# Strassen's seven products in the second matmul of an MLP too, in a two-layer diffusion step

## The chip, the cores and the metric

The kernel runs on one core of a Trainium2 chip. The metric is the device time of one execution in microseconds (us); lower is better. All inputs lie in HBM, all outputs end there.

## What is computed

Two trunk layers over 640 tokens (512 latent, 128 context) of width 1024. Layer 0 mixes by a convolution module and a bidirectional retention, layer 1 by grouped-query attention. Behind each mixer stands the part that the change touches:

```python
h = rmsnorm(x, norm_g[layer, 1]) * (1 + sc2) + sh2
x = x + g2 * (jnp.square(jax.nn.relu(h @ mlp_w1[layer])) @ mlp_w2[layer])
```

`mlp_w1` is 1024 x 4096 and `mlp_w2` 4096 x 1024, all in fp32. `sh2`, `sc2` and `g2` come from `silu(c) @ ada_w[layer]` and differ between latent and context tokens.

## The kernel before

Everything is held transposed: features on the 128 partitions, tokens along the free dimension, in two halves of 320 (`HALF`). An fp32 matmul is made of three in the reduced format `fp32r`: each operand is split into a high part (a rounding copy, by ScalarE) and a low part (value minus high part, by VectorE or GpSimd), and TensorE adds high x high, high x low and low x high in PSUM.

**Groups.** `mlp` works through the 4096 hidden features in 8 groups of 512 (`CYCLES`). A group's first matmul makes 512 hidden features from `h`, then ReLU and square, and its second matmul adds their product with 512 rows of `mlp_w2` to `x`. Groups 1 and 2 (`PLAIN`) do both in the ordinary way. In groups 3 to 8 the first matmul is a Strassen-like scheme (Winograd's form) of seven products of half-size blocks (`winograd`, line 1092 its matmul): the weights split in four blocks B11 to B22, the tokens in two halves, the 1024 input features in two. Three of its weight operands are blocks, four are sums of blocks (T1 to T4), made by VectorE in `t_sums` (line 2354) from the four loaded blocks; their high parts come from `split_product` (ScalarE, L1351) and their low parts from `t_lo` (VectorE, L2360). Each product is two output tiles of 128 x 320 with 4 chunks of 128 and 3 matmuls, 12 matmuls a tile. Products are combined in `combine` and `result` (VectorE, L2366); `product_1` (ScalarE, L1637) copies the first out of PSUM. `hidden_pair` (ScalarE, L1643 to L1651) does ReLU, square and high part per tile, `hidden_lo` (VectorE, L2298) the low part.

The second matmul of every group is plain: 16 output tiles x 4 chunks x 3 = 192 matmuls of 320 columns (`product`, line 665), each tile added to `xT` with the gate by `residual` (VectorE, L1876).

**Weights.** Raw weights come in blocks of 128 x 1024 fp32 (512 KB) by loads that SyncE issues (`load_mlp`, `load_tile`), into two pairs of buffers, `raw` and `raw_high`. `wH` and `wL` are rings of four blocks: the high part of a block may be written once TensorE is done with the block four before it. The order of `BLOCKS` is the order of use. Low parts of blocks that are not sums are made by GpSimd (`lo`, L1840), two instructions of 512 columns each.

**Order.** Each engine runs its own queue in written order and waits for semaphores: `acc_full` counts finished output tiles, `dve_free` tiles that VectorE has read, `wh_done`, `wl_done` and `t_low` weight parts. An instruction that waits holds up all behind it on its engine. In layer 0 TensorE also runs three strips of 32 small matmuls per group (`strips`, L784) for the modulation of later stages; each needs a load of 1 MB (`load_ada`), and VectorE's `modulation` finishes every second one.

The loop that sets the order of the second matmul:

```python
for q in range(4):
    w = weights((t + 2 + q // 2, q % 2), 256)
    for j in range(4):
        half, m = j // 2, j % 2
        free(4 * q + j)
```

Of the kernel before, what the change touches and what calls it, by code (L numbers as in the profile page):

```python
# [82 lines left out]
RAW_HIGH = [t for t in range(N_TILES) if t % 2 and t in TWO_RAW]  # L83
RAW_LOW = [t for t in range(N_TILES) if t not in RAW_HIGH]
RAW_AT = {t: (tiles, n) for tiles in (RAW_LOW, RAW_HIGH) for n, t in enumerate(tiles)}


def WINO_OF(t):

    for layer, t0 in enumerate((T_MLP0, T_MLP1)):  # L90
        c, b = divmod(t - t0, 4)
        if PLAIN <= c < CYCLES and b < 2:
            return WINO * layer + c - PLAIN, b
    return None


B11, T2, B21, T3, T1, T4, B22 = range(7)
T_ORDER, SUM_ORDER = (T2, T3, T1, T4), (T3, T1, T2, T4)
BLOCKS = []
for t_ in range(N_TILES):  # L100
    if WINO_OF(t_) is None:
        BLOCKS += [(t_, 0), (t_, 1)]
    elif WINO_OF(t_)[1] == 0:
        BLOCKS += [("p", WINO_OF(t_)[0], i_) for i_ in range(7)]
BLOCK_AT = {key: n for n, key in enumerate(BLOCKS)}
POOL_LO = [key for key in BLOCKS if (key[2] not in T_ORDER if key[0] == "p" else key[0] not in DVE_LO)]
# [11 lines left out]
G_CYCLE = [24 * c + 6 * max(c - PLAIN, 0) for c in range(CYCLES + 1)]  # L118
# [6 lines left out]
A_MLP1 = A_QKV + 30  # L125
def F_AT(c, half, k):

    if c == 0:
        return 4 * half + k
    if c < PLAIN:  # L130
        return 4 * (k // 2) + 2 * half + k % 2
    return k + (4 if (half == 0) == (k < 2) else 0)


F_GROUP = [{F_AT(c, half, k): (k, half) for half in range(2) for k in range(4)} for c in range(CYCLES)]

# [8 lines left out]
V_WO = V_MLP0 + 16 * CYCLES  # L145
# [79 lines left out]
def hybrid_step(nc, x_prompt, x_sample, state_ret, cache_k, cache_v, ada_w, even_w_in, even_w_out, final_g,  # L225
# [3 lines left out]
    with ctx:  # L229
# [3 lines left out]
        def place(name, shape, dt=F32):  # L233
# [70 lines left out]
        here[0] = arena  # L304
        fH = place("fH", [P, 4, T], F32R)
        fL = place("fL", [P, 4, T], F32R)
        fr = place("fr", [P, 4, HALF])
        fs = place("fs", [P, 2, HALF])
# [3 lines left out]
        p1 = place("p1", [P, 2, HALF])  # L312
        u2 = place("u2", [P, 2, HALF])
        u3 = place("u3", [P, 2, HALF])
        s1_raw = nc.alloc_sbuf_tensor_at("s1_raw", [P, 4, HALF], F32, offset=mlp_end)
        s23 = place("s23", [P, 2, 2, 4, HALF], F32R)
        s4_raw = place("s4_raw", [P, 4, HALF])
        s4 = place("s4", [P, 2, 4, HALF], F32R)
        t1_raw = nc.alloc_sbuf_tensor_at("t1_raw", [P, 1024], F32, offset=here[0] - 4 * 3840)
# [3 lines left out]
        t3_raw, t2_raw, t4_raw = (nc.alloc_sbuf_tensor_at(f"t{n}_raw", [P, 1024], F32, offset=norm_buffers + 4096 * j)  # L323
                                  for j, n in enumerate((3, 2, 4)))
# [44 lines left out]
        t_raw = {T1: t1_raw, T2: t2_raw, T3: t3_raw, T4: t4_raw}  # L369
        s_hi = {1: hH[:, 0:4, 0:HALF], 2: s23[:, 0, 0], 3: s23[:, 1, 0], 4: s4[:, 0]}  # L370
        s_lo = {1: hL[:, 0:4, 0:HALF], 2: s23[:, 0, 1], 3: s23[:, 1, 1], 4: s4[:, 1]}
# [10 lines left out]
        def raw(t):  # L382

            return raw_high if t % 2 and t in TWO_RAW else raw_low
# [11 lines left out]
        def sem(name):  # L396
# [7 lines left out]
        raw_in = [sem("raw_in0"), sem("raw_in1")]  # L404
        raw_high_in = [sem("raw_high_in0"), sem("raw_high_in1")]
# [33 lines left out]
        t_sum, t_low = sem("t_sum"), sem("t_low")  # L439
        p1_done, u2_done, u3_done, w5_done, c_done = (sem("p1_done"), sem("u2_done"), sem("u3_done"), sem("w5_done"),  # L440
                                                     sem("c_done"))
# [14 lines left out]
        def raw_landed(t, j):  # L456

            return (raw_high_in if RAW_AT[t][0] is RAW_HIGH else raw_in)[j]

        def wait_raw(engine, t, j):  # L460

            engine.wait_ge(raw_landed(t, j), 16 * (RAW_AT[t][1] + 1))

        def wait_low(engine, *key):

            if key[0] == "p" and key[2] in T_ORDER:
                engine.wait_ge(t_low, 4 * key[1] + T_ORDER.index(key[2]) + 1)
# [7 lines left out]
        def wait_raw_free(engine, t, j):  # L475

            if WINO_OF(t) is None:
                wait_low(engine, t, j)
            else:
                s, odd = WINO_OF(t)  # L480
                engine.wait_ge(t_sum, 4 * s + 4)
                if (odd, j) != (1, 0):
                    wait_low(engine, "p", s, (B11, B21, None, B22)[2 * odd + j])
# [5 lines left out]
        def _(sp):  # L489
# [3 lines left out]

            def load_tile(t, halves, js=(0, 1)):

                for j, src in enumerate(halves):
                    tiles, at = RAW_AT[t]
                    if j in js:
                        if at:
                            wait_raw_free(sp, tiles[at - 1], j)  # L500
                    else:
                        continue
                    n = src.shape[2]
                    sp.dma_start(raw(t)[:, j, :].rearrange("p (k n) -> p k n", n=n), src).then_inc(raw_landed(t, j), 16)
# [69 lines left out]
            def load_mlp(layer, first_tile):  # L574
# [15 lines left out]

                w1(0)
# [2062 lines left out]
```

## Time and profile before

| | |
|---|---|
| median of 3 runs | 1569.06 us (1567.79 to 1569.22) |
| profiled execution: its time and span | 1567.7 us |
| mean granted TensorE clock | 0.997 of full speed |
| TensorE, VectorE, ScalarE, GpSimd busy | 1546.4, 989.9, 625.7, 487.8 us |
| HBM traffic | 162.23 MB, 103 GB/s in the mean |

The span runs from the first to the last instruction of one profiled execution; the profiled execution's own time is this span, 1567.7 us, 1.4 below the median of the runs. Matmuls overlap: a single one shows as 309 ns while the next starts 147 ns after it, so the cost of a stage is read from its length, not from the sum of its instructions. Likewise a VectorE or ScalarE instruction may start somewhat before its predecessor's shown end.

### The profile page before, as it was taken

The numbers are of one execution on the slowest core, as the hardware profiler recorded it, in microseconds if no ns is written. First come the engines' busy times: TensorE is split into PE (matmuls) and PEld (weight loads), VectorE is DVE, ScalarE is ACT, GpSimd is POOL, SyncE is SP. The second block draws the span as 40 slices with busy tenths as digits, with TensorE's granted clock in tenths as the row PEclk, the third lists the DMA queues.
The fourth block names the chain that finished last, engine by engine and source line by source line (L and its number), as shares of the span: only waits on it lengthen the run. The fifth ranks groups of instructions, "written<-read, shape, count | busy, mean of one in ns | idle before, by whom it ended". The sixth has DMA issues, their size and how long they took to land.

```text
span 1567.7 us, 28794 instructions
## 1 busy us (share of the span) xinstructions
PE 1546.4 (99%) x11994; PEld 1513.1 (97%) x11994; DVE 989.9 (63%) x1831; ACT 625.7 (40%) x1152; POOL 487.8 (31%) x350
## 2 busy tenths in 40 slices
PE   8999999999999999999999999999999999999998
PEld 7999999999999999999999999999999999999998
DVE  5348678675774755565555888773675755556555
ACT  5323333344432344234235534652443334523443
POOL 0233313314222343143235253101333344324431
PEclk9999999999999999999999999999999999999999
DMA  9454333313243334344253121001221232223212
GB/s 330 154 180 151 116 114 123 101 55 108 81 151 116 124 124 139 116 135 149 95 161 134 35 81 61 28 2 54 81 81 55 67 108 68 82 68 102 74 54 82
DMA packets 133410, 162.23 MB, mean 103 GB/s; under 512 B 4640, under 2 KB 108064, under 8 KB 133280
## 3 DMA queue, kind: packets, MB, share of 16 engines
q1 hardware_dynamic: 132048, 159.34, 31.5%
q8 instruction: 95, 1.56, 0.4%
q10 hardware_dynamic: 1232, 1.05, 0.2%
q14 instruction: 35, 0.29, 0.1%
HBM read 156.44 MB, written 3.93 MB: 102 GB/s over the span
## 4 chain that ended last, share of the span: by engine, by line
PE 90%; DVE 6%; ACT 2%; issue 1%; DMA 0%; POOL 0%; DVEq 0%; ACTq 0%
PE ps L665 59%; PE ps L1092 19%; PE ps L784 3%; PE ps L1284 2%; PE ps L1232 1%; DVE ps L1915 1%; PE ps L921 1%; PE ps L954 1%; DVE hL L1926 1%; PE ps L870 1%; DVE ps L1905 1%; PE ps L950 1%; DVE amx L2512 1%; ACT wH L1328 1%; PE ps L1259 1%
## 5 line engine op out<-in xcount | busy, mean ns | idle before, releaser
L1840 POOL TENSOR_TENSOR wL<-raw,wH 128x512 fp32r<-128x512 f32 x212 | 314.6, 1509 | 709.5 <-ACT wH L1328 514.7
L665 PE MATMUL ps<-fH,wH 128*128 128x320 f32 x1024 | 318.5, 311 | 0.2 <-DVE fL L2298 0.2
L665 PE MATMUL ps<-fL,wH 128*128 128x320 f32 x1024 | 316.3, 309 | 0.0
L665 PE MATMUL ps<-fH,wL 128*128 128x320 f32 x1024 | 316.3, 309 | 0.0
L1876 DVE SCALAR_TENSOR_TENSOR xT<-ps,modT,xT 128x192 f32<-128x192 f32 (+1 forms) x456 | 183.3, 434 | 192.0 <-PE ps L665 190.1
L1840 POOL TENSOR_TENSOR wL<-raw_high,wH 128x512 fp32r<-128x512 f32 x124 | 164.2, 1349 | 338.5 <-ACT wH L1351 209.6
L665 PE MATMUL ps<-hH,wH 128*128 128x320 f32 x704 | 221.1, 314 | 1.9 <-DVE hL L1926 1.3
L665 PE MATMUL ps<-hH,wL 128*128 128x320 f32 x704 | 217.5, 309 | 0.0
L665 PE MATMUL ps<-hL,wH 128*128 128x320 f32 x704 | 217.5, 309 | 0.0
L665 PEld LDWEIGHTS ps<-fH,wH 128*128 128x128 f32 x1024 | 192.3, 188 | 3.4 <-DVE xT L1876 1.2
L665 PEld LDWEIGHTS ps<-fL,wH 128*128 128x128 f32 x1024 | 192.3, 188 | 0.1
L665 PEld LDWEIGHTS ps<-fH,wL 128*128 128x128 f32 x1024 | 192.3, 188 | 0.0
L665 PE MATMUL ps<-wH,hH 128*128 128x256 f32 x560 | 162.1, 289 | 2.4 <-DVE hL L1926 2.1
L665 PE MATMUL ps<-wL,hH 128*128 128x256 f32 x560 | 158.3, 283 | 0.0
L665 PE MATMUL ps<-wH,hL 128*128 128x256 f32 x560 | 158.3, 283 | 0.0
L1351 ACT ACTIVATE wH<-t_raw 128x1024 fp32r<-128x1024 f32 x48 | 50.8, 1059 | 226.6 <-PE ps L665 172.9
L665 PEld LDWEIGHTS ps<-hH,wH 128*128 128x128 f32 x704 | 132.2, 188 | 6.4 <-DVE hL L1926 2.8
L665 PEld LDWEIGHTS ps<-hL,wH 128*128 128x128 f32 x704 | 132.2, 188 | 0.2
L665 PEld LDWEIGHTS ps<-hH,wL 128*128 128x128 f32 x704 | 132.1, 188 | 0.0
L2298 DVE TENSOR_TENSOR fL<-fs,fH 128x320 fp32r<-128x320 f32 x128 | 92.0, 749 | 58.8 <-ACT fH L1651 52.3
L1092 PE MATMUL ps<-s,wH 128*128 128x320 f32 x576 | 127.9, 310 | 0.0
L1092 PE MATMUL ps<-hH,wH 128*128 128x320 f32 x384 | 119.3, 311 | 0.0
(271 smaller groups left out, 3095.4 us busy)
## 6 DMA issues: line engine op xcount, KB each, us to landing
ada<-in_ada_w SPq DMA_DIRECT2D x40, 1024.0 KB, 5.3
raw<-in_mlp_w SPq DMA_DIRECT2D x64, 512.0 KB, 3.7
raw_high<-in_mlp_w SPq DMA_DIRECT2D x64, 512.0 KB, 3.8
raw<-in_even_w_in SPq DMA_DIRECT2D x28, 512.0 KB, 5.9
pre_w<-in_ada_w SPq DMA_DIRECT2D x16, 512.0 KB, 8.9
raw<-in_odd_w_qkv SPq DMA_DIRECT2D x10, 512.0 KB, 3.5
raw<-in_even_w_out SPq DMA_DIRECT2D x8, 512.0 KB, 3.5
raw<-in_odd_w_o SPq DMA_DIRECT2D x6, 512.0 KB, 3.4
```

Source lines behind the costliest of these rows:

```text
L665: last = nc.tensor.matmul(ps[:, bank, 0:width], a_, b_, start=(k == 0 and p_ == 0), stop=(k == nk - 1 and p_ == 2))
L784: last = nc.tensor.matmul(ps[32 * j:32 * j + 32, B_ADA, 0:P], siluc[:, 4 * part + k, :], by_lane[:, j], start=(part == 0 and k == 0), stop ...
L870: last = nc.tensor.matmul(ps[:, GATE_BANKS[n], 0:HALF], a_, b_, start=(k == 0 and p_ == 0), stop=(k == KC - 1 and p_ == 2))
L921: return nc.tensor.matmul(ps[:, bank, at:at + RV], kd_nat[:, r, tile, :], v_nat[:, tile, :], start=True, stop=True)
L950: last = nc.tensor.matmul(out, prob[:, cs], v_nat[:, tile, :], start=True, stop=ctx_)
L954: last = nc.tensor.matmul(out, qdec[:, r, cs], S[:, r, n, :], start=False, stop=(r == 1))
L1092: last = nc.tensor.matmul(ps[:, bank + m, 0:HALF], a_, b_, start=(k == 0 and p_ == 0), stop=(k == 3 and p_ == 2))
L1284: last = nc.tensor.matmul(ps[:, 6, cs], va[:, vt, kv * P:(kv + 1) * P], pT[:, h % 2, n, cs], start=(n == 0), stop=(n == 4))
L1351: nc.scalar.activation(wH[:, BLOCK_AT["p", s, i] % 4, :], src, ACT.Copy).then_inc(wh_done, 1)
L1840: last = nc.gpsimd.tensor_tensor(wL[:, at % 4, cs], raw(t)[:, j, cs], wH[:, at % 4, cs].bitcast(F32), ALU.subtract)
L1876: last = nc.vector.scalar_tensor_tensor(out=x, in0=ps[:, n % 4, c0 - half * HALF:c0 - half * HALF + w_], scalar=modT[:, gate_at + k, which ...
L2298: nc.vector.tensor_tensor(fL[:, k, halfcols(half)], fs[:, n % 2, :], fH[:, k, halfcols(half)].bitcast(F32), ALU.subtract).then_inc(f_ready, 1)
```

## The change

In groups 3 to 7 of both layers (`W2`) the second matmul becomes seven products too (`second_strassen`). The group's 512 hidden features and the 1024 outputs are halved, and so are the tokens. Four weight sums T1 to T4 of `mlp_w2` blocks are made by VectorE (`q_add`), four sums of hidden blocks S1 to S4 likewise (`operand_sum`), and each of the seven hidden operands gets a high part (`operand_hi`, ScalarE) and a low part (`operand_lo`, VectorE) in a ring `fx` of three. All instructions on hidden blocks now work on 640 columns at once. Products are accumulated on each other in the same PSUM bank: TensorE adds products one to four in banks 0 to 3, and VectorE reads each bank in between (`product_out`), before the next product is added to it. For one token half the reading goes straight to `xT`, for the other into a buffer `held` over all five groups, which group 8 adds to `xT` (`held_out`).

The first matmul of groups 3 to 8 (`first_strassen`) accumulates its products likewise. Its weight sums are no longer made by VectorE: GpSimd issues loads that add to what lies in the buffer (`accum_op`), five per group, T2 and T4 in a buffer of their own, T1 and T3 in raw buffers. All low parts of second-matmul blocks, and those of B11, T2 and T3 of the first, are GpSimd's; T1, B22, B21 and T4 are VectorE's. The raw buffers become one ring of four within the MLPs. `operand_hi` of the fourth to seventh operand waits until TensorE is done with the operand three before.

```diff
-B11, T2, B21, T3, T1, T4, B22 = range(7)
+W2 = range(PLAIN, CYCLES - 1)
+B11, T2, T3, T1, B22, B21, T4 = range(7)
+Q_ORDER = (B11, T2, T3, T4, T1, B22, B21)
+P_DVE = (T1, B22, B21, T4)
...
+            def block_product(key, width, nk, bank, m, operand, opens):
+                w = weights(key, width)
+                for k in range(nk):
+                    (aH, aL), (bH, bL) = [x[:, k, m * P:(m + 1) * P] for x in w], operand(k)
+                    for p_, (a_, b_) in enumerate(((aH, bH), (aH, bL), (aL, bH))):
+                        last = nc.tensor.matmul(ps[:, bank, 0:HALF], a_, b_, start=(opens and k == 0 and p_ == 0),
+                                                stop=(k == nk - 1 and p_ == 2), skip_group_check=not opens)
+                last.then_inc(acc_full, 1)
...
+            def second_strassen(layer, c, v, part):
...
+                def begin(i, name):
+                    wait_low(pe, "q", s, i)
+                    pe.wait_ge(x_low, 7 * s + name + 1)
+                begin(B11, A11_)
+                for m in range(4):
+                    if m < 3:
+                        pe.wait_ge(c_done, 6 * s1 + 3 + m)
+                    one(B11, A11_, m, m)
+                begin(T2, S2_)
+                for m in range(4):
+                    pe.wait_ge(dve_free, v + m + 1)
+                    one(T2, S2_, m, m, False)
...
+            # ScalarE, a group with both matmuls by seven products
+                        partials(c, p1, 1, p1_done)
+                        split_product("p", s, B22, g + 2)
+                        partials(c, u2, 3, u2_done)
+                        split_product("p", s, B21, g + 4)
+                        partials(c, u3, 5, u3_done)
+                        split_product("p", s, T4, g + 6)
+                        split_product("q", s2, B11, g + 8)
+                        hidden_block(c, F11)
+                        operand_hi(c, A11_)
+                        split_product("q", s2, T2, g + 10)
+                        hidden_block(c, F21)
+                        operand_hi(c, S3_)
+                        hidden_block(c, F22)
+                        split_product("q", s2, T3, g + 12)
+                        operand_hi(c, S2_)
+                        hidden_block(c, F12)
+                        split_product("q", s2, T4, g + 14)
+                        operand_hi(c, A22_)
...
+                        for n, i in enumerate((B11, T2, T3, T1)):
+                            split_product("p", s + 1, i, g + 30 + 4 * n)
...
+            # GpSimd
+            def add_block(s, out, row, col, done):
+                layer, c = s // WINO, PLAIN + s % WINO
+                src = mlp_w1[layer, 512 * row:512 * (row + 1), 512 * c + 256 * col:512 * c + 256 * (col + 1)]
+                nc.gpsimd.dma_start(out.rearrange("p (k n) -> p k n", n=256), src.rearrange("(k p) n -> p k n", p=P),
+                                    accum_op=ALU.add).then_inc(done, 16)
+            def t1_ends(s):
+                wait_raw(pool, "p", s, T1)
+                add_block(s, raw(("p", s, T1)), 0, 0, t1_added)
...
+                    after[before[0]] = lambda s=s: t2_begins(s)
+                    after[before[1]] = lambda s=s: t2_ends(s)
+                    after[before[2]] = lambda s=s: t3_ends(s)
+                    after["p", s, B11] = lambda s=s: t1_ends(s)
+                    after["p", s, T2] = lambda s=s: t4_ends(s)
...
+            # VectorE
+                def strassen_cycle(c):
+                    t_lo(s, T1)
+                    t_lo(s, B22)
                     modulate(c, 0)
+                    t_lo(s, B21)
+                    q_add(s2, T1)
                     t_lo(s, T4)
+                    combine(c, F11, 0)
+                    combine(c, F11, 1)
+                    modulate(c, 1)
+                    q_add(s2, T2)
+                    combine(c, F21, 0)
+                    operand_lo(c, A11_)
+                    combine(c, F21, 1)
+                    q_add(s2, T3)
+                    combine(c, F22, 0)
+                    operand_sum(c, S3_)
+                    combine(c, F22, 1)
+                    q_add(s2, T4)
+                    operand_lo(c, S3_)
+                    operand_sum(c, S2_)
+                    operand_sum(c, S1_)
+                    operand_lo(c, S2_)
+                    for m in range(4):
+                        product_out(c, 0, m)
+                    product_out(c, 1, 0)
+                    operand_lo(c, A22_)
...
```

Here `q_add` of T4 waits for `wait_raw` of B21 and for GpSimd's low part of T2 (`wait_low(dve, "q", s2, T2)`), since it overwrites the buffer of T2. `F11`, `F21`, `F22`, `F12` are the four blocks of hidden features by token half.

## Rows read from the trace of the kernel before

**Rows 1.** The page: busy time, share of the span and instructions; granted clock by slices.
```profile
PE 1546.4 (99%) x11994; PEld 1513.1 (97%) x11994; DVE 989.9 (63%) x1831; ACT 625.7 (40%) x1152; POOL 487.8 (31%) x350
...
PEclk9999999999999999999999999999999999999999
```

**Rows 2.** The page: chain that ended last, shares by line.
```profile
PE ps L665 59%; PE ps L1092 19%; PE ps L784 3%; PE ps L1284 2%; PE ps L1232 1%; DVE ps L1915 1%; PE ps L921 1%; PE ps L954 1%; DVE hL L1926 1%; PE ps L870 1%; DVE ps L1905 1%; PE ps L950 1%; DVE amx L2512 1%; ACT wH L1328 1%; PE ps L1259 1%
```

**Rows 3.** Chain in order of time, one group of layer 0: start, us, what.
```profile
678.54 14.07 PE ps L665 x96
692.62 1.01 PE ps L784 x32
693.63 14.28 PE ps L665 x96
```

**Rows 4.** The same, one group of layer 1.
```profile
1237.52 24.64 PE ps L1092 x168
1262.15 28.28 PE ps L665 x192
```

**Rows 5.** Busy time by stage; columns: stretch, length, engines, clock, DMA share, GB/s.
```profile
651.50:678.54 27.04, 27.04 (x234) 26.26 (x234) 14.87 (x26) 15.01 (x27) 8.12 (x6) 1.00 0.41 141
622.13:651.50 29.37, 29.37 (x226) 28.98 (x226) 16.64 (x33) 6.45 (x10) 10.70 (x8) 1.00 0.41 123
...
1262.15:1290.43 28.28, 28.28 (x195) 28.28 (x195) 16.31 (x32) 6.51 (x11) 10.72 (x8) 1.00 0.30 93
1237.52:1262.15 24.63, 24.63 (x169) 24.53 (x169) 14.23 (x23) 14.87 (x27) 8.13 (x6) 1.00 0.23 76
```

**Rows 6.** VectorE in order of time: start, us, instruction; 1024, 1280, 320 columns.
```profile
602.08 1.22 DVE L2360 TENSOR_TENSOR wL<-t_raw,wH 128x1024 fp32r<-128x1024 f32 x1
603.43 0.49 DVE L2366 TENSOR_TENSOR u<-ps,p 128x320 f32<-128x320 f32 x1
...
630.97 0.55 DVE L1876 SCALAR_TENSOR_TENSOR xT<-ps,modT,xT 128x320 f32<-128x320 f32 x1 [1.08 <-PE ps L665]
...
1205.35 1.48 DVE L2318 TENSOR_TENSOR s_raw<-hH,hL 128x1280 f32<-128x1280 f32 x1
```

**Rows 7.** ScalarE: a high part of a block, and two copies of 320 columns.
```profile
617.57 1.05 ACT L1328 ACTIVATE wH<-raw 128x1024 fp32r<-128x1024 f32 x1
...
623.20 0.81 ACT L1647 ACTIVATE fs<-fr 128x320 f32<-128x320 f32 x2
```

**Rows 8.** GpSimd in order of time: pairs of halves, alone and beside VectorE.
```profile
1182.14 2.56 POOL L1840 TENSOR_TENSOR wL<-raw_high,wH 128x512 fp32r<-128x512 f32 x2 [4.50 <-ACT wH L1328]
...
645.64 3.07 POOL L1840 TENSOR_TENSOR wL<-raw,wH 128x512 fp32r<-128x512 f32 x2 [12.76 <-ACT wH L1351]
```

**Rows 9.** GpSimd and VectorE in the same stretch, subtractions with both inputs in SBUF.
```profile
1196.90 6.37 POOL L1840 TENSOR_TENSOR wL<-raw,wH 128x512 fp32r<-128x512 f32 x4 [12.21 <-ACT wH L1328]
...
1199.07 1.54 DVE L2307 TENSOR_TENSOR fs<-fr 128x320 f32<-128x320 f32 x1 [1.23 <-ACT fr L1628]
...
1202.04 2.58 DVE L2318 TENSOR_TENSOR s_raw<-s_raw 128x1280 f32<-128x1280 f32 x1
1204.54 0.48 DVE L2307 TENSOR_TENSOR fs<-fr 128x320 f32<-128x320 f32 x1
```

**Rows 10.** TensorE's next tile starts, and VectorE reads the tile before.
```profile
606.68 0.46 PE L1092 MATMUL ps<-s,wH 128*128 128x320 f32 x2
...
606.95 0.49 DVE L2366 TENSOR_TENSOR fr<-ps,p 128x320 f32<-128x320 f32 x1 [0.87 <-PE ps L1092]
```

**Rows 11.** Loads: count, KB each, median us to landing; and SyncE's issue.
```profile
ada<-in_ada_w SPq DMA_DIRECT2D x40, 1024.0 KB, 5.3
raw<-in_mlp_w SPq DMA_DIRECT2D x64, 512.0 KB, 3.7
...
raw_high<-in_even_w_in SPq DMA_DIRECT2D x4, 512.0 KB, 9.0
...
613.28 0.37 SPq L504 DMA_DIRECT2D raw_high<-in_mlp_w  x1
```

More of the change, by code:

```diff
@@ L82 @@
 TWO_RAW = {T_GATE + 1, T_VAL + 1, *range(T_WC - 2, T_QKV + 2), *range(T_WO + 2, N_TILES)}
[L83 to L94, printed above, removed]
@@ new lines @@
+for t_ in range(N_TILES):
+    layer_ = 0 if T_MLP0 <= t_ < T_QKV else 1
+    c_, b_ = divmod(t_ - (T_MLP0, T_MLP1)[layer_], 4)
+    if not (T_MLP0 <= t_ < T_QKV or T_MLP1 <= t_) or b_ < 2 and c_ < PLAIN or b_ > 1 and c_ not in W2:
+        BLOCKS += both(t_)
+        RAW_SEQ += both(t_)
+    elif b_ == 0:
+        BLOCKS += [("p", WINO * layer_ + c_ - PLAIN, i_) for i_ in range(7)]
+        RAW_SEQ += [("p", WINO * layer_ + c_ - PLAIN, i_) for i_ in (B11, T3, T1, B22, B21)]
+    elif b_ == 2:
+        BLOCKS += [("q", len(W2) * layer_ + c_ - PLAIN, i_) for i_ in Q_ORDER]
+        RAW_SEQ += [("q", len(W2) * layer_ + c_ - PLAIN, i_) for i_ in (B11, T1, B22, B21)]
@@ L125 @@
 A_MLP1 = A_QKV + 30
+F_CYCLE = {0: 0, 1: 8, CYCLES - 1: 16}
+F_LAYER = 24
 def F_AT(c, half, k):
@@ L492, in cols, with load_raw @@
                 return w[k0 * P:(k0 + nk) * P, bass.ds(c0, n)].rearrange("(k p) n -> p k n", p=P)
+            def load_raw(key, src):
+                if RAW_PREV[key]:
+                    wait_raw_free(sp, RAW_PREV[key])
+                sp.dma_start(raw(key).rearrange("p (k n) -> p k n", n=src.shape[2]), src).then_inc(raw_landed(key)[0], 16)
             def load_tile(t, halves, js=(0, 1)):
[L496 to L504, printed above, removed]
+                for j in js:
+                    load_raw((t, j), halves[j])
             def k8(w, c0, row0=0):
@@ new lines, in partial, with partials @@
+                def partial(c, m, out, groups, done):
+                    act.wait_ge(acc_full, g0 + G_CYCLE[c] + groups + m)
+                    nc.scalar.activation(out[:, m, :], ps[:, 6 + m, 0:HALF], ACT.Copy).then_inc(done, 1)
+                def partials(c, out, groups, done):
+                    s, s2 = WINO * layer + c - PLAIN, len(W2) * layer + c - PLAIN
+                    if out is p1 and c == PLAIN:
+                        act.wait_ge(s_ready, 4 * layer + 4)
+                    elif out is p1:
+                        act.wait_ge(c_done, 6 * s)
+                    elif out is u3 and c - 1 in W2:
+                        act.wait_ge(x_low, 7 * (s2 - 1) + S4_ + 1)
+                    for m in range(2):
+                        partial(c, m, out, groups, done)
@@ new lines, in combine @@
+                def combine(c, b, m):
+                    s = WINO * layer + c - PLAIN
+                    bank, add, done, op = ((m, u3, u3_done, ALU.subtract), (m, u2, u2_done, ALU.subtract),
+                                           ((2, 5)[m], p1, p1_done, ALU.add))[b]
+                    dve.wait_ge(acc_full, g0 + G_CYCLE[c] + 7 + 2 * b + m)
+                    dve.wait_ge(done, 2 * s + 1 + m)
+                    nc.vector.tensor_tensor(fq[:, b, m, :], ps[:, bank, 0:HALF], add[:, m, :], op).then_inc(c_done, 1)
@@ new lines, in held_out @@
+                def held_out(k):
+                    for c0, w_, which in SEGS[1]:
+                        x = xT[:, k, c0:c0 + w_]
+                        nc.vector.scalar_tensor_tensor(out=x, in0=held[:, k, c0 - HALF:c0 - HALF + w_],
+                                                       scalar=modT[:, gate_at + k, which:which + 1], in1=x,
+                                                       op0=ALU.mult, op1=ALU.add)
+                def strassen_cycle(c):
+                    s, s2 = WINO * layer + c - PLAIN, len(W2) * layer + c - PLAIN
+                    t_lo(s, T1)
+                    t_lo(s, B22)
```

607 lines of the change are left out of this document (388 added, 219 removed).

## The prediction

> **What bounds the kernel now.** I read the busy shares and the clock first, then the chain that ended last, then that chain group by group, then the tables by stage, and only then single queues. TensorE is busy for 99% of the span at the full granted clock, 2.4 GHz [rows 1], and 78% of the chain are matmuls of the two product helpers [rows 2]. An MLP group of layer 0 is TensorE from end to end: 27.04 us for the first matmul (168 matmuls and two 1.01 us strips), 29.37 for the second (192 and one strip), 56.4 in all [rows 3, 5]; in layer 1 it is 24.63 + 28.28 = 52.9 [rows 4]. In both TensorE is busy for the whole length [rows 5]: it waits for nothing. VectorE is busy 14.9 to 16.6 us per half group, ScalarE 15.0 and 6.5, GpSimd 8.1 and 10.7, the DMA engines 0.41 in layer 0 and 0.23 to 0.30 in layer 1 [rows 5]. So TensorE work taken out is time, as far as the others keep up; the prediction is about them. The profiled span, 1567.7, lies 1.4 us below the median of the runs, 1569.06; I subtract from the median.
>
> **What is removed on TensorE.** A matmul of 320 columns costs 24.63 / 168 = 0.147 us [rows 4]. A second matmul by seven products is 7 x 4 output tiles x 2 chunks x 3 = 168 matmuls, not 192: 24 fewer, 3.52 us, in ten groups: 35.2 us. The 0.1 to 0.2 us by which 192 matmuls exceed 192 x 0.147 (14.28 against 14.08 for 96 [rows 3]) I let go too: 1.6 in all. The first matmul keeps 14 groups of 12 matmuls (1.76 us each); the second gets 28 of 6 (0.88 each, 3.52 per product). Floor with all else hidden: 1569.1 - 36.8 = 1532.3, some 24.64 + 24.64 = 49.3 us per group in layer 1 and 52.3 in layer 0.
>
> **What the other engines get.** Prices: VectorE 1.22 us for 1024 columns and 1.48 for 1280, both inputs in SBUF, so 0.82 for 640; 0.49 for 320 out of PSUM; 0.55 for a residual update; each starts about 0.07 before its predecessor's end [rows 6]. ScalarE 1.05 for 1024, 0.455 for 320, so 0.72 for 640 [rows 7]. GpSimd 1.27 for half a weight block [rows 8].
> - VectorE per group: four low parts and four sums of second weights (8 x 1.15), four operand sums and seven operand low parts (11 x 0.75), six combinations and 28 products out (34 x 0.44): 32.4 us plus 0.5 of modulation, of 49.3. The sums T1 to T4 of the first matmul (4 x 1.15) go. It fits as a sum.
> - ScalarE: 14 x 0.96 + 6 x 0.37 + 15 x 0.64 = 25.3 us. It fits.
> - GpSimd: ten blocks, not seven: 25.4 us, plus five issues of adding loads. The first to last of these ten have about 12 block times of 3.52 us = 42.
> - A bank is read while three other banks are written (2.64 us); a read takes 0.5, so accumulating on the read bank costs nothing while VectorE is not over 2 us late.
> - In the last group the held half goes out as 16 small updates, some 5.5 us of VectorE beside a first matmul in which it has over 9 us free: nothing. The swapped halves of the S operands, the ring of raw buffers, the rope loads' earlier release and the other banks have the same cover; I cost them at nothing, and at up to 1 us in all if not.
>
> **The wait that I expect.** VectorE's 320-column subtraction takes 0.48 us, but 1.54 beside GpSimd's, and the 1280-column one 2.58, not 1.48; GpSimd's four halves then take 6.37, not 5.1 [rows 9]. They take turns: one half block of GpSimd (1.1 us of waiting) between any two such VectorE instructions. Instructions that read PSUM and one SBUF operand don't wait. Until now the two hardly meet; the changed group has 19 such VectorE instructions against 20 halves, and seven of the nineteen stand in one chain. I walked the queues in their written order with these prices, 0.27 us from a group's end to its reader [rows 10], 1.3 us per issue on GpSimd. Time from the start of a layer 1 group: the second phase starts at 24.6, product two (T2 with S2) is due at 28.2. The F22 tiles end at 21.1, but VectorE is late by then: the low part of A11 waited for a half block (18.2 to 19.0), T3's sum ends at 20.6, S3's sum waits for a half and runs 21.6 to 22.4, so F22 is combined at 22.9. Relu and square: 24.6. T4's sum needs GpSimd's low part of T2 (23.6): to 24.9. Low part of S3: 25.6. Sum S2: 26.4. GpSimd's half; sum S1, queued ahead: 27.4 to 28.2. GpSimd's half; low part of S2: 30.0. Product one's first bank is read behind it, until 30.4, and the second product must wait for that too: 30.4 against 28.2 is 2.3 us (unrounded). The same walk without turns has S2 ready at 26.5, 1.6 us early, and stalls nowhere. In layer 0, with VectorE's modulation (0.5) in the same queue every other group, it gives 2.3 to 2.6. Ten groups: 5 x 2.3 + 5 x 2.45 = 23.8.
>
> On this the Trainium skill has a rule (SBUF - State Buffer, "Who interferes with whom"): a VectorE instruction with two SBUF inputs contends with a GpSimd instruction that reads SBUF, and who holds the port blocks the other. It speaks against this change, and the rows agree: 0.48 against 1.54. Without the rule the time would be the floor.
>
> **The adding loads.** No row has a load issued by GpSimd or one that adds; the bounds are rows of others. *Issue*: from below SyncE's 0.37 us [rows 11]; from above a slowed pair of halves, 3.07 [rows 8]; I take 1.3, the nearest, one GpSimd instruction. *Landing from the start of the issue*: plain 512 KB take 3.7, or 9.0 in the crowded head stage, a 1 MB load 5.3 [rows 11]. An adding load handles its bytes twice, so 1.3 + 5.3 = 6.6, between 3.7 and 1.3 + 9.0 = 10.3. What waits: ScalarE's high part of T1 (first matmul) stands ahead of its copies of product one, and those free the bank for TensorE's third tile. T1's add is issued when the low part of B11 is done, some 4 to 6 us before the new group; it may land up to 2 us into it. Landing at 6.6 costs nothing in the walk, 8 costs 0.9 per layer 1 group, 10 costs 2.9 (layer 0 1.2, its strip being cover). GpSimd's queue waits too, before three of the five adds: for the plain load under T3 and under T1, which SyncE may issue only when the low part of the block that held the buffer is done, and for the first add under T2. In the walk these have landed 0.5 to 3 us before GpSimd comes to them. SyncE passes two MB loads of the modulation in layer 0 between them; each waits for a strip that TensorE has run by then, and none of its waits is longer than one block time. All this leans on GpSimd being on time: a late block delays the next raw load, and that the add. Traffic: a group loads 15 half megabytes, not 8; layer 0's 7.3 MB at share 0.41 become 11, share 0.62, and 0.8 if added bytes count twice. That is below one but stretches landings.
>
> The Trainium skill says that a DMA's add needs two source reads, which halves the rate (Collectives: The Full Stack, "The bandwidth ceiling"), and gives about 1 us to the first byte for loads issued by GpSimd (DMA: Bandwidth & Descriptors, "Specifications"). No row here shows either; they would leave my landing, and lower the issue to about 1.0.
>
> By issue (and landing) the stalls per group in layer 1 and 0 come to: 0.4 (3.7): 1.2 and 1.9; 1.3 (6.6): 2.3 and 2.45; 2.0 (6.6): 2.9 and 3.8; 2.5 (8): 5.6 and 5.1; 3.0 (9): 10.2 and 8.6.
>
> **The sum.** 1569.1 - 36.8 + 23.8 = 1556.1. I say 1556.
>
> **Rivals.**
> 1. *Forecast*: turns at the port, late S2, 1.5 to 3 us in each of ten groups: 1547 to 1563. Chance 0.40.
> 2. *All hidden*: the turns are shorter than in rows 9 or fall elsewhere; the walk without them has 1.6 us to spare. For it: TensorE has no waits now. Against: rows 9. 1532 to 1547, centre 1534. Chance 0.27.
> 3. *GpSimd becomes the bound* (slower). Five issues and ten blocks in one queue; from its T4 block (free to start 3.2 us into the second phase) to the low part of T3 it has 28.5 us for seven blocks and four issues: 7 x 2.6 + VectorE's turns of 4 + 4 issues. It decides from an issue of 2.1 us or a landing over 9: then T1 lands late, ScalarE stands, and TensorE waits in every group. At 2.5 and 8: 1569.1 - 36.8 + 53.5 = 1586; at 3.0 and 9: 1626. For it: 3.07 us is a price that pairs of halves reach. Against: issues elsewhere cost 0.37. Chance 0.26, and 0.07 more for cases between, 1563 to 1572.
>
> **Numbers.** A measurement of this kernel tells about 0.2%, 3 us, from no change. Faster by more (under 1566): 0.40 + 0.27 + 0.02 = 0.69; within: 0.06; slower: 0.25. For 8 in 10 the range takes in all of the first two and the slow case up to an issue of 2.4: 1533 to 1582; the forecast's own is 1547 to 1563.
>
> **What would show it.** Second matmul, layer 1: 168 matmuls and one gap of 2 to 2.5 us ahead of product two's first tile, released by VectorE's reading of product one (line of the product read); its low part of S2 ends 5 us after the phase starts. VectorE's 640-column subtractions spread from 0.82 to 1.9 us. GpSimd busy over 25 us per group, each issue near 1.3. If the gap is not there, the turns were mispriced; if a gap stands ahead of the third tile of a group, released by ScalarE's copy, it is rival 3. A TensorE wait on weights in most groups, or on a read in the later products, would make the working wrong.

## The result

Before: 1569.1 us. After: 1624.6 us median (1609.1 to 1635.8), ratio 1.033 [1.029, 1.036]: slower by 3.3%, outside the predicted range (1533 to 1582), 69 us above the forecast of 1556. Here and below the medians are of all runs and the ratios of the fast ones alone; without the slow run of 1635.8 us the median after is 1620.0. The profiled execution took 1620.0 us, of which its span, the stretch from the first to the last instruction, is 1617.8. (In its later executions the kernel before takes 1.8 us more than its span as well, so the 1567.7 us of its profile are a span and not also a time; the prediction subtracts from the median, and nothing in it changes.)

The page of the kernel after: busy time, the queue of the loads that GpSimd issues (packets, MB, share), the chain by engine, and two rows of issues (KB each, median us to landing).
```profile
PE 1540.4 (95%) x11754; PEld 1498.7 (93%) x11754; DVE 1128.9 (70%) x1829; ACT 683.0 (42%) x1140; POOL 648.8 (40%) x470
...
q0 software_dynamic: 31680, 31.46, 13.1%
...
PE 68%; DVE 15%; ACT 6%; POOL 4%; DMA 4%; issue 3%; DVEq 0%; SPq 0%; ACTq 0%
...
t_first<-in_mlp_w POOLq DMA_DIRECT2D x36, 512.0 KB, 6.2
raw_high<-in_mlp_w POOLq DMA_DIRECT2D x14, 512.0 KB, 7.7
```
Against [rows 1, 2]: 240 matmuls are gone, as said, but TensorE's busy time fell by 6.0 us only, not by 35, and its share from 99 to 95%. The span less TensorE's busy time, 21.3 us before (1567.7 - 1546.4), is now 77.4. VectorE has 15% of the chain.

Layer 1, kernel after; columns as in [rows 5]: a whole group, then the first matmul of the next one, and the stretch of its second in which a long stall lies.
```profile
1325.20:1380.60 55.40, 52.05 (x340) 51.14 (x339) 42.54 (x54) 26.91 (x35) 34.49 (x26) 0.97 0.64 143
1380.60:1405.20 24.60, 24.21 (x165) 23.98 (x164) 15.78 (x16) 12.39 (x18) 8.23 (x7) 1.00 0.64 153
1405.20:1435.70 30.50, 22.91 (x137) 22.42 (x136) 27.22 (x32) 13.34 (x17) 20.83 (x16) 0.89 0.46 104
```
A group takes 55.1 to 60.1 us; it took 52.9 [rows 4, 5], and 49.3 was the floor. TensorE, which had no gap in [rows 4], now has them in every group. Two of them, kernel after: TensorE's first matmuls behind a gap.
```profile
1410.91 0.53 PE L1180 MATMUL ps<-fx,wH 128*128 128x320 f32 x2 [2.16 <-DVE held L2657]
...
1424.50 0.90 PE L1180 MATMUL ps<-fx,wH 128*128 128x320 f32 x2 [5.43 <-DVE xT L2652]
```
The first stands where the forecast put it, ahead of product two, released by VectorE's read of product one: 2.1 to 2.2 us in each of five groups of layer 1, 1.8 to 3.3 in layer 0. The second is not in the forecast: 54 matmuls, that is nine tiles, lie between the two, so it stands inside product four, ahead of its second tile, and what releases it is VectorE's read of product three. It is this long in one group only; the other groups have gaps of 0.3 to 2.0 us at their later products, mostly inside product three or four. GpSimd and VectorE beside the long one (GpSimd's halves one by one):
```profile
1414.56 1.29 POOL L2063 DMA_DIRECT2D t_first<-in_mlp_w  x1
1415.38 1.81 POOL L2043 TENSOR_TENSOR wL<-raw,wH 128x512 fp32r<-128x512 f32 x1
1416.63 1.79 POOL L2043 TENSOR_TENSOR wL<-raw,wH 128x512 fp32r<-128x512 f32 x1
...
1421.57 1.72 POOL L2043 TENSOR_TENSOR wL<-raw_high,wH 128x512 fp32r<-128x512 f32 x1
1423.62 1.32 POOL L2063 DMA_DIRECT2D raw<-in_mlp_w  x1 [0.33 <-DMA raw<-in_mlp_w]
```
```profile
1416.01 0.53 DVE L2652 SCALAR_TENSOR_TENSOR xT<-ps,modT,xT 128x320 f32<-128x320 f32 x1
1416.47 7.51 DVE L2643 TENSOR_TENSOR fx<-fq,fx 128x640 fp32r<-128x640 f32 x1
1423.91 1.91 DVE L2652 SCALAR_TENSOR_TENSOR xT<-ps,modT,xT 128x320 f32<-128x320 f32 x4
```
GpSimd issues a load and then runs six half blocks, one starting every 1.25 us. VectorE's subtraction, 0.81 us of work, takes 7.51: it gets through only after the last half ends at 1423.29 and GpSimd pauses for 0.33 us. In [rows 9] it got its turn after one half.

The longest wait of this kind lies outside the ten changed groups, in the second matmul of group 2 of layer 0, where GpSimd issues the first of its loads. GpSimd runs eight halves and two issues there without a pause, and VectorE's subtraction of 1280 columns (1.48 us of work) takes 11.92; TensorE waits 5.26 us for the `xT` update queued behind it. VectorE and TensorE:
```profile
517.14 11.92 DVE L2580 TENSOR_TENSOR s<-s_raw,s 128x1280 fp32r<-128x1280 f32 x1
529.57 0.63 PE L756 MATMUL ps<-fH,wH 128*128 128x320 f32 x1 [5.26 <-DVE xT L2124]
```

After such a gap TensorE is slow as well. Kernel after, TensorE alone: stretch, length, busy, granted clock, DMA share, GB/s. The last stretch lies in another group, right behind a gap of 2.16 us, whose first matmuls follow.
```profile
1416.00:1419.00 3.00, 3.00 (x21) 1.00 0.79 110
1419.00:1424.00 5.00, 0.07 (x1) 0.97 0.93 246
...
1426.00:1428.00 2.00, 2.00 (x9) 0.50 1.11 219
...
1432.00:1436.00 4.00, 4.00 (x30) 1.00 0.06 11
...
1356.00:1358.00 2.00, 2.00 (x9) 0.50 0.41 86
```
```profile
1355.35 0.80 PE L1180 MATMUL ps<-fx,wH 128*128 128x320 f32 x2 [2.16 <-DVE held L2657]
```
The granted clock falls to 0.50 of full speed (1.2 GHz) behind the gap and is back at 2.4 GHz by 1432. It does so behind short gaps too: from 540 us to the end of the last group the kernel after has thirteen gaps of 1.8 us and more, and behind twelve of them (all but the 2.16 us at 1410.91) stands a stretch at 0.50, 44 us in all; behind the gaps up to 1.5 us there is none. Another 3 us stand behind the gap of 5.26. The mean over the run is 0.982, against 0.997 before.

### The profile page after: what moved, and what is told of

The parts are those of the page before. It is cut to its first block, busy times and chain, and to the rows that moved or that the text cites. A ratio compares the mean times of both kernels' runs of the same rounds, so it can differ in the third digit from the quotient of the medians.

```text
span 1617.8 us, 28358 instructions
## 1 busy us (share of the span) xinstructions
PE 1540.4 (95%) x11754; PEld 1498.7 (93%) x11754; DVE 1128.9 (70%) x1829; ACT 683.0 (42%) x1140; POOL 648.8 (40%) x470
## 3 DMA queue, kind: packets, MB, share of 16 engines
q0 software_dynamic: 31680, 31.46, 13.1%
## 4 chain that ended last, share of the span: by engine, by line
PE 68%; DVE 15%; ACT 6%; POOL 4%; DMA 4%; issue 3%; DVEq 0%; SPq 0%; ACTq 0%
PE ps L756 40%; PE ps L1180 17%; POOL wL L2043 4%; DVE fx L2643 3%; PE ps L875 2%; PE ps L1428 2%; DMA raw_high<-in_mlp_w 2%; ACT wH L1490 2%; DVE u L2634 1%; DMA raw<-in_mlp_w 1%; PE ps L1376 1%; ACT fx L1814 1%; DVE ps L2163 1%; PE ps L1012 1%; PE ps L1045 1%
## 5 line engine op out<-in xcount | busy, mean ns | idle before, releaser
L1180 PE MATMUL ps<-fx,wH 128*128 128x320 f32 x1120 | 265.3, 326 | 44.4 <-DVE held L2657 24.1
L2043 POOL TENSOR_TENSOR wL<-raw_high,wH 128x512 fp32r<-128x512 f32 x128 | 183.1, 1524 | 219.2 <-ACT wH L1472 126.1
L1180 PEld LDWEIGHTS ps<-fx,wH 128*128 128x128 f32 x1120 | 199.3, 201 | 52.7 <-issue 27.6
L756 PE MATMUL ps<-hH,wL 128*128 128x320 f32 x704 | 217.6, 309 | 0.0
L756 PE MATMUL ps<-hL,wH 128*128 128x320 f32 x704 | 217.5, 309 | 0.0
L1180 PE MATMUL ps<-fx,wL 128*128 128x320 f32 x560 | 180.6, 322 | 0.0
L2124 DVE SCALAR_TENSOR_TENSOR xT<-ps,modT,xT 128x192 f32<-128x192 f32 (+1 forms) x216 | 85.9, 432 | 89.2 <-PE ps L756 88.7
L756 PE MATMUL ps<-fH,wH 128*128 128x320 f32 x384 | 120.7, 314 | 6.3 <-DVE xT L2124 5.3
L756 PE MATMUL ps<-fL,wH 128*128 128x320 f32 x384 | 119.2, 311 | 0.0
L1180 PE MATMUL ps<-hL,wH 128*128 128x320 f32 x384 | 119.2, 310 | 0.0
L1180 PE MATMUL ps<-hH,wL 128*128 128x320 f32 x384 | 119.2, 310 | 0.0
L756 PE MATMUL ps<-fH,wL 128*128 128x320 f32 x384 | 119.2, 310 | 0.0
```

Of the source, the lines that this page charges most:

```text
L756: last = nc.tensor.matmul(ps[:, bank, 0:width], a_, b_, start=(k == 0 and p_ == 0), stop=(k == nk - 1 and p_ == 2))
L1180: last = nc.tensor.matmul(ps[:, bank, 0:HALF], a_, b_, start=(opens and k == 0 and p_ == 0), stop=(k == nk - 1 and p_ == 2), skip_group_ch ...
L2043: last = nc.gpsimd.tensor_tensor(wL[:, at % 4, cs], source(key)[:, cs], wH[:, at % 4, cs].bitcast(F32), ALU.subtract)
L2124: last = nc.vector.scalar_tensor_tensor(out=x, in0=ps[:, n % 4, c0 - half * HALF:c0 - half * HALF + w_], scalar=modT[:, gate_at + k, which ...
```

## The experiments

My theory at the start: a load that GpSimd issues leaves its queue without pauses, and VectorE then waits for the whole run, not for one half (A). Rivals: the adding makes the loads slow (B); the port is overbooked, whoever issues (C). All ratios are to the kernel before, 1569.0 to 1569.5 us beside them. The edits are shortened.

**1. Not adding.**
```
-  nc.gpsimd.dma_start(out, src, accum_op=ALU.add).then_inc(done, 16)
+  nc.gpsimd.dma_start(out, src).then_inc(done, 16)
```


> The changed kernel with its five loads per group issued by GpSimd as before, but as plain loads that overwrite (T1 to T4 of the first matmul are then single blocks, not sums). Theory A (a load issued by GpSimd puts its queue into a mode in which the following half blocks run without a gap and VectorE's two-input instructions wait for the whole run, up to 7 us): nothing changes, 1610 to 1635, VectorE's 640-column low parts still reach 7 us. Rival B (the adding itself is slow: landings of 6.2 to 7.7 us hold up ScalarE and TensorE): landings fall to about 4.5, time 1585 to 1600. Rival C (the port is simply overbooked, whoever issues): 1610 to 1635 like A.

1616.1 us, 1.030 [1.024, 1.035]; the loads land in 4.2 and 6.0 us (medians) instead of 6.2 and 7.7. GpSimd, VectorE and TensorE in one group of it:
```profile
1409.28 0.77 POOL L2063 DMA_DIRECT2D t_first<-in_mlp_w  x1
1410.07 1.31 POOL L2043 TENSOR_TENSOR wL<-raw,wH 128x512 fp32r<-128x512 f32 x1
1411.32 1.31 POOL L2043 TENSOR_TENSOR wL<-raw,wH 128x512 fp32r<-128x512 f32 x1
...
1411.19 7.02 DVE L2642 TENSOR_TENSOR fx<-fq,fx 128x640 fp32r<-128x640 f32 x1
...
1418.73 0.64 PE L1180 MATMUL ps<-fx,wH 128*128 128x320 f32 x1 [4.92 <-DVE xT L2651]
```
The issue is shorter (0.77, not 1.29), the halves are of normal length (1.31), and VectorE still waits for the whole run of six, in each group of layer 1 (and in two of layer 0), where the kernel after has it in one. B explains at most 8.5 us. One run behind an issue did take turns here, four halves from 515.3 us, all but the first 2.5 us long, at the place where the kernel after has its 11.92. So an issue ahead of a run is not enough by itself.

**2. SyncE issues the same loads**, each behind the same wait, also not adding; GpSimd has its low parts alone.
```
+  sp.wait_ge(t24_in, 16 * (s + 1))
+  sp.dma_start(t24_first, p_block(c, 0, 1)).then_inc(t24_added, 16)
...
-  if key in after:
-      after[key]()
```


> The same five loads per group, same bytes and order, but plain (not adding; T1 to T4 of the first matmul are single blocks) and issued by SyncE; GpSimd only makes low parts. A: the turns alternate again, half a block (1.1 us) per wait; VectorE's low parts stay under 2.1 us; 1550 to 1568. B: 1585 to 1600, equal to the kernel whose loads GpSimd issues without adding. C: over 1600, as the port carries the same instructions.

1552.6 us, 0.989 [0.988, 0.991]. C falls: VectorE's and GpSimd's subtractions are all there. Its page, busy time:
```profile
PE 1513.0 (98%) x11754; PEld 1476.5 (95%) x11754; DVE 1073.4 (69%) x1829; ACT 684.7 (44%) x1140; POOL 605.8 (39%) x410
```
The gap of one group in it, and GpSimd and VectorE in the same group:
```profile
1359.82 0.53 PE L1193 MATMUL ps<-fx,wH 128*128 128x320 f32 x2 [1.01 <-DVE held L2668]
...
1363.46 1.89 POOL L2056 TENSOR_TENSOR wL<-raw,wH 128x512 fp32r<-128x512 f32 x1
1365.31 1.29 POOL L2056 TENSOR_TENSOR wL<-raw,wH 128x512 fp32r<-128x512 f32 x1
...
1365.37 1.91 DVE L2654 TENSOR_TENSOR fx<-fq,fx 128x640 fp32r<-128x640 f32 x1
```
The same back-to-back halves now let VectorE in after one (1.91 us). With the same 11754 matmuls TensorE is busy 27.4 us less than in the kernel after. Most of that is the clock: here no gap of the groups is followed by half clock, and the 48 us at 0.50 of the kernel after cost up to 24; the rest would be waits too short to show as idle time (an estimate). So the 69.1 us between the two spans (1617.8 - 1548.7) are 27.4 of longer matmuls and 41.7 of gaps. The gaps are 13.7 us more ahead of product two (24.7 in the ten groups, here 11.0), 18.4 at the later products (here none over 0.25), 5.3 in group 2 of layer 0, 2.9 at ScalarE's copy of product one, and 0.9 at a load of the modulation. The only gap over 0.25 us in groups 3 to 7 of layer 1 is 1.0 us in each, ahead of product two.

**3. No extra loads at all** (T1 to T4 are plain single blocks).


> The changed kernel without the five adding loads (T1 to T4 of the first matmul are the single blocks that SyncE loads; no issue on GpSimd, no landing to wait for, 2.6 MB less traffic per group). A: as with SyncE's issues or slightly less, 1548 to 1565: what is left is the alternating wait ahead of product two, about 2.3 us per group. B: all its cost is gone, 1545 to 1560. C: over 1595.

1551.8 us, 0.989 [0.987, 0.991], as the second: 31 MB of traffic cost 0.8 us, within the scatter.

**4. GpSimd waits for the end of each half**, the kernel otherwise as changed.
```
+  pool.wait_ge(wl_done, POOL_AT[key] - 1)
   for c0 in (0, 512):
       last = nc.gpsimd.tensor_tensor(...)
+      last.then_inc(low_half, 1); pool.wait_ge(low_half, n)   # first half
```


> The changed kernel whole, but GpSimd waits for the end of each of its half blocks before it starts the next (its own semaphore), so that no two overlap. A: VectorE gets its turn after every half, its longest low part falls from 7.5 to about 2.1 us; the gaps ahead of product two shrink little, those of 1 to 5.4 us ahead of product three go; 1560 to 1590. B: GpSimd gets slower by its waits, landings unchanged: 1620 to 1650. C: 1610 to 1640.

1607.5 us, 1.023 [1.021, 1.026], above what I expected: the long waits are gone (VectorE's 640-column low parts take 1.34 us in the mean and 2.8 at most, in the kernel after 1.62 and 7.5), but the time fell by 17 us only. A new gap of 3.1 to 3.5 us stands in each group of layer 1 (0.6 to 2.7 in four of layer 0), at ScalarE's copy of product one of the first matmul. Its chain (start, us, what):
```profile
1418.04 8.26 DMA raw<-in_mlp_w
...
1426.38 0.04 ACT wH L1491
...
1427.91 4.22 PE ps L1181 x18
```
T1's adding load lands late; ScalarE waits for it in front of the copy, TensorE for the copy. That is rival 3 of the prediction, at an issue of 1.3 us.

**5. One wait behind each issue**, between the two halves that follow it (60 waits).
```
+  elif drained and c0 == 0:
+      last.then_inc(low_half, 1)
+      pool.wait_ge(low_half, drained)
```


> The whole changed kernel; only the first half block that follows one of GpSimd's load issues is waited for before the second (one wait per issue, 60 in all, not one per half block). If the long waits of VectorE come from a queue of GpSimd that an issue sets overlapping and that stays so until GpSimd pauses, one pause is enough: no VectorE subtraction of two SBUF inputs above 2.7 us (7.5 before), the gap ahead of product two 1.75 us as with a wait at every half, and, since GpSimd loses about 0.35 x 5 instead of 0.35 x 10 to 15 us a group, the gap at ScalarE's copy of product one falls from 3.3 us to under 1.5: 1560 to 1585, centre 1570. If the issue's own descriptor work takes the port whatever follows it, the waits stay at 4 to 8 us and the time at 1600 to 1625.

1595.3 us, 1.017 [1.015, 1.020], 10 us above the expected interval. GpSimd behind an issue, and TensorE at the copy:
```profile
1398.19 1.29 POOL L2067 DMA_DIRECT2D t_first<-in_mlp_w  x1
1399.01 1.80 POOL L2044 TENSOR_TENSOR wL<-raw,wH 128x512 fp32r<-128x512 f32 x1
1400.89 1.77 POOL L2044 TENSOR_TENSOR wL<-raw,wH 128x512 fp32r<-128x512 f32 x1
1402.62 1.30 POOL L2044 TENSOR_TENSOR wL<-raw,wH 128x512 fp32r<-128x512 f32 x1
...
1422.12 0.54 PE L1181 MATMUL ps<-s,wH 128*128 128x320 f32 x2 [2.68 <-ACT p L1774]
```
The mechanism is as expected: one wait restores the turns for the whole run. No such VectorE instruction spans more than one whole half any more; the longest subtraction or sum takes 3.5 us, above the 2.7 expected. What I mis-sized is GpSimd's lateness: blocks cost 3.1 to 3.5 us with fair turns, so in layer 1 the copy's gap is still 2.2 to 2.8 us and not under 1.5, and half clock follows three of these five.

**6. VectorE's queue reordered in the version of experiment 2**: F22's combinations ahead of T3's and S3's sums, T4's sum behind S2's low part.


> The kernel whose extra loads SyncE issues without adding (the sums T1 to T4 of the first matmul are left out), and in VectorE's queue T3's sum goes behind the F22 combinations and S3's sum, T4's sum behind S2's low part. If the 1.0 us ahead of product two is the turns at the port on S2's chain (T3's sum at 2.0 us and S3's at 1.5 stand ahead of F22's combination, S2's low part takes 1.77), the gap falls to 0 to 0.4 us: 1552.6 - 10 x 0.8 = 1544 (1541 to 1548). If the gap is ScalarE's order (T3's high part ahead of S2's), it stays at 0.9 to 1.1: 1552.

1577.6 us, 1.005 [1.003, 1.006]: 24 to 25 us worse than without it. VectorE, and TensorE:
```profile
1376.77 2.28 DVE L2619 TENSOR_TENSOR t_second<-raw_high,t_second 128x1024 f32<-128x1024 f32 x1
...
1379.60 0.53 PE L1193 MATMUL ps<-fx,wH 128*128 128x320 f32 x2 [2.58 <-DVE held L2668]
```
S2 was ready 0.2 us before product two was due, but T4's sum, with a turn 2.28 us, stood between it and the read of product one for which TensorE waits as well.

**7, 8. That order and T3's low part on VectorE, with and without the waits of experiment 5.**


> The whole changed kernel with three edits: one wait behind each issue of GpSimd as before, VectorE's queue reordered as in the SyncE version, and the low part of T3 of the first matmul given to VectorE. GpSimd has 9 blocks a group instead of 10 (-3.1 us), so T1's adding load goes out some 3 us earlier and the gap at ScalarE's copy is gone; the gap ahead of product two is 0.3 to 1.0 us: 1545 to 1562, centre 1552. If GpSimd's queue is still the bound (an issue and its load under it too late), 1562 to 1580.

> The same as the combined version without the waits behind GpSimd's issues. If the overlap after an issue is what starves VectorE, its long waits stay (a run of GpSimd's halves behind the issue at T4 is still four to six long): a gap of 3 to 6 us in most groups and half clock after it, 1585 to 1620. If the waits of VectorE had to do with how full GpSimd's queue was, nine blocks instead of ten remove them: under 1565.

With: 1607.6 us, 1.024 [1.023, 1.026], wrong, by the same mistake in the order (3.1 us ahead of product two in each group of layer 1, 3.3 to 4.0 in layer 0). Without: 1633.1 us, 1.041 [1.037, 1.046], above the interval too, and the 7.51 us wait is there, in one group, with nine blocks in GpSimd's queue as with ten. Between the two only the 60 waits differ: they are worth 25 us.

**9, 10. ScalarE's high part of T1 behind its copies of product one**, with the waits of experiment 5; in the first also a second order for VectorE (T4's sum early, S1's sum behind product one's reads).
```
   partials(c, p1, 1, p1_done)
+  if c > PLAIN:
+      split_product("p", s, T1, g)
...
-  for n, i in enumerate((B11, T2, T3, T1)):
+  for n, i in enumerate((B11, T2, T3)):
```


> The first two of these three edits, VectorE's queue as in the changed kernel. 1595.3 less the gap at ScalarE's copy (2.6 us in five groups of layer 1, about 1.5 in four of layer 0) and less the half clock that follows it (PE busy 1526.5 against 1513): 1595 - 19 - 12 = 1564 (1558 to 1572), with 1.6 us ahead of product two as before. If the gap only moves (to T1's weights or T3's), 1580 to 1595.

> The whole changed kernel with three edits, each against one measured gap: one wait behind each issue of GpSimd (the long waits of VectorE); ScalarE's high part of T1 of the first matmul behind its copies of product one, not ahead (the 2.2 to 2.8 us gap at that copy: it waits for T1's adding load, which lands 7.8 us after its issue); VectorE's queue with the F22 combinations ahead of T3's and S3's sums, S2's sum and low part ahead of S1's sum, and T4's sum well ahead of product one's reads (in the first reordering it stood between S2's low part and those reads and cost 2.3 us a group). Expected: no gap at the copy, 0.3 to 0.6 us ahead of product two, clock 0.997: 1541 to 1556, centre 1546. If GpSimd's queue itself is the bound (rival 3 of the prediction), the gap moves to a wait for weights or to T3 and the time stays over 1570.

1577.4 us, 1.006 [1.004, 1.008], without the second order: the gap at the copy is gone and 18 us with it, 5 us short of the expected interval; up to 0.8 us stands at later combinations in some groups. With the second order 1585.7 us, 1.011 [1.009, 1.012], where 1541 to 1556 was expected: in layer 1 the gap ahead of product two fell to 0.74 us, and 1.42 appeared inside product three, ahead of its third tile.

**11. The second order in the version of experiment 2.**


> The kernel whose extra loads SyncE issues without adding (sums T1 to T4 of the first matmul left out), with the second reordering of VectorE's queue. If the remaining 1.0 us ahead of product two is VectorE's turns with GpSimd on S2's chain, as the prediction had it, it falls to 0.2 to 0.4: 1552.6 - 7 = 1545 (1542 to 1549). If product one's reads or ScalarE's order set it, 1550 or more.

1561.4 us, 0.995 [0.994, 0.997]; not the 1545 expected. Ahead of product two 0.38 us, ahead of the third tile of product three 0.69: together the 1.0 there was, and TensorE busy 7 us longer at the same clock, so with small waits. Neither order took the turns away; an instruction moved off S2's chain takes its turn in front of a read.

**12. VectorE makes the sums T1 and T4**, only T2 and T3 keep adding loads, T2's first issue goes behind a low part after which GpSimd idles, with the waits of 5 and ScalarE's order of 10.
```
+  def p_add(s, i):      # T1: raw(T1) + raw(B11); T4: t24_first + raw(B21)
+      nc.vector.tensor_tensor(out, out, b, ALU.add).then_inc(done, 1)
...
-  after["p", s, B11] = lambda s=s: t1_ends(s)
-  after["p", s, T2] = lambda s=s: t4_ends(s)
```


> The whole computation, three of GpSimd's five issues a group left: the sums T1 and T4 of the first matmul are made by VectorE (1.22 us each, in the first half of the group, where it idles 3 to 5 us at a time and GpSimd has nothing to do), only T2 and T3 by adding loads, and T2's first issue stands behind the low part of the second matmul's T2 instead of ahead of it; with the wait behind each issue and ScalarE's copies ahead of T1's high part. If what is left of the loss lies in GpSimd's issues (ahead of T2's low part: 1.6 instead of 1.0 us ahead of product two; T1 landing late: 0.3 to 0.8 us at the combinations), it goes: 1577.4 - 10 x 0.6 - 10 x 0.5 - 3 for the modulation's loads = 1563 (1555 to 1570), that is faster than before by 0.4%. If VectorE's two more sums cost as much as they save, or the loads of layer 0 set the time, 1572 to 1582.

1555.6 us, 0.992 [0.990, 0.993]: the whole computation, faster than both kernels. That it comes out at the forecast's figure is chance: it is another kernel. Against experiment 10 it changes several things at once (24 of the 60 issues gone, one moved, VectorE's sums), so what each is worth is not shown. Its busy time, one group's gap, and one whole group as a stretch:
```profile
PE 1514.9 (97%) x11754; PEld 1478.4 (95%) x11754; DVE 1094.9 (70%) x1853; ACT 682.8 (44%) x1140; POOL 640.4 (41%) x446
```
```profile
1366.18 0.53 PE L1184 MATMUL ps<-fx,wH 128*128 128x320 f32 x2 [1.00 <-DVE held L2669]
```
```profile
1338.00:1388.60 50.60, 49.60 (x339) 49.33 (x338) 40.63 (x56) 27.78 (x36) 33.68 (x24) 1.00 0.56 136
```
A group of layer 1 takes 50.6 us with one gap of 1.0, as where SyncE issues. One further gap, in layer 0, 5.4 us and nearly 3 ahead of the same matmul in the kernel after, is a modulation load that SyncE issues behind a raw load that it can't issue yet:
```profile
819.32 0.37 SPq L545
...
819.73 8.19 DMA ada<-in_ada_w
```

## Why the prediction was wrong

- **What is removed on TensorE**: right. 1546.4 to 1513.0 at the same clock (experiment 2) is 33.4 us for 240 matmuls; 35.2 was the term, 36.8 with what I let go at the tiles.
- **Prices of single instructions**: right. Issue 1.29 (1.3 said), landing 6.2 and 7.7 in the median (6.6 said), VectorE 0.81 and 1.22, its reads 0.48.
- **The wait that I expect**: right in place and kind, wrong in size. Where SyncE issues, S2's chain follows the walk step by step, but for one turn: S1's sum ran before GpSimd's next half (until 26.8 us of the group, not from 27.4 to 28.2), and the gap is 1.0 us, not 2.3. The 2.15 us of the kernel after look like a hit, and so do the ten gaps' 24.7 us against the 23.8 of the sum, but both are luck: T3's sum took 3.90 us there, behind an issue, where the walk had none of that. The sum in the kernel after, and where SyncE issues:
```profile
1399.75 3.90 DVE L2608 TENSOR_TENSOR raw_high<-t_second,raw_high 128x1024 f32<-128x1024 f32 x1
...
1349.81 2.00 DVE L2619 TENSOR_TENSOR raw_high<-t_second,raw_high 128x1024 f32<-128x1024 f32 x1
```
- **"One half block of GpSimd between any two such VectorE instructions"**: this step failed. I read it off [rows 9], and no load of GpSimd's own stands in them. Behind an issue VectorE can wait for the whole run, 7.5 us and once 11.9 (shown by experiments 1, 2 and 5, and by 8 against 7). Of the traces of all runs, none without an issue in GpSimd's run has a two-SBUF instruction of VectorE that spans more than one whole half; the kernels whose GpSimd issues and doesn't wait have up to six. The walk added 1.3 us to GpSimd's queue for an issue and nothing to VectorE's. So VectorE read the products late, and TensorE waited 18.4 us at later products, where the prediction had nothing; it had named a wait on a read there as the sign that its working is wrong.

The Trainium skill (SBUF - State Buffer, "SBUF: two separate sides") says that who holds the shared pair keeps it for the whole instruction. The rows agree in kind where no issue precedes (1.91 us); behind an issue VectorE waited for a run of six instructions, which that page doesn't say.

- **The adding loads cost nothing**: wrong, and hidden in the kernel after. Rival 3 was to decide from an issue of 2.1 us or a landing over 9. With VectorE's turns restored it decides at 1.29 and 7.8: T1's add goes out about 3 us before the new group, not 4 to 6 (1412.8 against 1415.9 in experiment 5), because T3's add and its wait stand ahead and a block takes 3.1 to 3.5 us, and it flies together with T3's. In the kernel after the gap at the copy is at most 0.4 us in layer 1 (1.4 in layer 0), since GpSimd, which doesn't yield, is fast. Rival 3's 1626 us, at an issue of 3.0 us and a landing of 9, meets the measured time by luck; the issue is 1.29.
- **Clock**: no term. The working had only waits; of the 69 us up to 24 are TensorE at half clock behind them (48 us at 0.50).
- **Traffic**: right, nothing that can be measured (experiment 3).

The sum with measured terms, between profiled executions: 1567.7 - 33.4 + 11.0 (the ten gaps ahead of product two) + 2.0 (a modulation load of layer 0) + 1.4 (not followed up) = 1548.7, where SyncE issues. From there to the kernel after: 27.4 of longer matmuls, most of it half clock, and 41.7 of gaps: 1617.8. The median lies 6.8 above that, 2.2 of it between span and time of the same execution, the rest the scatter of the four. I took 1556 for the likeliest by one mechanism too large (turns) and one absent (starvation). No rival had VectorE starved by an issue; the slower one had the right engine, not the right victim.

Left open: why a run behind an issue isn't interrupted. My first idea was that the halves overlap, since the first starts 0.8 us into an issue of 1.29 and they show 1.7 to 1.8 us at a pitch of 1.25; experiment 1 excludes that and the adding (issue and halves end to end, 1.31 at a pitch of 1.25, as everywhere), experiment 5 shows that one wait of GpSimd on its own result ends it; what it resets no row shows, nor why the run from 515.3 us in experiment 1 took turns behind its issue.

## What to carry to other kernels

Price an instruction that an engine has never issued in the trace by what it does to the neighbours on a shared resource too, not only by its own length, and say in the rivals that no row shows this. Where VectorE works on two SBUF operands, give plain loads to SyncE; if GpSimd must issue them, let it wait once behind each issue, or issue where it idles next (the second was tried only together with other edits, in experiment 12). A gap of TensorE of 1.8 us and more was in the kernel after nearly always worth more than its length: add the half-clock stretch behind it.

## What I had not expected of the hardware

- Behind a load that GpSimd issues, its uninterrupted run of half blocks kept VectorE's two-SBUF subtractions out for 7.0 to 7.5 us (0.81 of work) and once for 11.92 (1.48 of work), through two further issues; without the issue, the same run let it in after one half (1.91 us). 60 waits in GpSimd's queue: 25 us.
- A load of 512 KB issued by GpSimd takes its queue for 0.77 us plain and 1.29 adding; all sixty loads together make 8640 packets plain and 31680 adding, for the same 31.46 MB.
- The clock behind a gap: after the 1.0 us gaps of experiments 2, 3 and 12 and the 1.65 of experiment 1 it stayed at 1.00; after 4.9 to 5.5 us (ten gaps outside the head of the kernel, and the 5.26) TensorE ran at 0.50 for another 3 to 6 us every time. Between, length alone doesn't decide: after 2.13 to 2.16 us it fell in four of five groups of layer 1 in the kernel after, after 2.58 in seven of ten gaps of experiment 6, and after 1.82 once and once not (kernel after, experiment 5).
